# Sample page gathers of the latent attention: the wait on the scores moved from the sixth key chunk to the ninth

## The chip, the cores and the metric

One core of one Trainium2 chip runs the whole kernel. The metric is device time in microseconds (us) of one launch; three runs of the kernel before gave 2556.86, 2560.39 and 2561.03 us, median 2560.39 us. TensorE's granted clock is 0.998 of its full 2.4 GHz over the profiled execution.

## The reference, cut to what matters

One inference step of a two-layer decoder: a prompt group of 256 tokens and a sample group of 8 sequences with 8 new tokens each. Every layer has two feed-forward blocks around a token mixer with three branches: a delta-rule recurrence, a dilated window attention, and a multi-head latent attention. The change touches the third branch, for the samples. Each sample has 2048 past tokens, kept as 16 pages of 128 rows in a pool; a row is 256 latent numbers and 32 rotated key numbers, and a page table says which pages a sample owns.

```python
ckv = cache_mla_ckv[l][page_table].reshape(db, past_len, KV_LORA)       # gathered latents
krope = cache_mla_krope[l][page_table].reshape(db, past_len, DROPE)     # gathered rotary keys
s = (einsum('bqhc,blc->bhql', ql, ckv_all) + einsum('bqhr,blr->bhql', qr, krope_all)) * scale
p = softmax(where(key_rows <= rows, s, -inf))
o_lat = einsum('bhql,blc->bqhc', p, ckv_all)
```

Everything is float32. The latents serve twice: transposed as keys of the scores, and as they stand as values.

## The kernel before, in words

Each engine has a program of its own, written out by hand; they meet only in semaphores. `S["ml_mm"]`, `S["ml_pv"]` and the like are counters, `then_inc` adds to one when an instruction is done, and `wait_ge` holds an engine until a counter has reached a value. No planner reorders anything.

The stage of the samples' latent attention (`ml_sample` in the programs of TensorE, ScalarE and VectorE) loops over the 8 samples, here called sample 0 to 7. For sample b TensorE does in order:

- `ml_scores(b)`, the scores of 64 queries against 2048 keys, in nine chunks `d` of the contracted width: 0 to 3 use the low half of the latents (`KTl`), 4 to 7 the high half (`KTh`), 8 the rotary keys (`KRT`). A chunk is eight calls on 32-row by 64-column tiles, which the trace shows as 16 instructions. All of them accumulate in four PSUM banks. `ml_mm` is raised twice for each sample, after chunk 5 and after chunk 8.
- `by_channel(b-2)`, `ml_own_tokens(b+1)` (the scores against the sample's own new tokens, which raises `ml_s`), `values(b-1)` (32 matmuls of the shares of the last sample with its gathered latents; raises `ml_pv`), and `shares(b, ...)`, which transposes the exponentials of sample b.

VectorE does for sample b: `maximum(b)`, whose large reduction of the scores (L2771) waits for `ml_mm` to be 2(b+1), so for chunk 8, and is followed by four small steps (L2772 to L2775); `own_scores(b+1)` (L2764, waits for `ml_s`); `keys(b+1, 0)`, two transposes (L2716) of the next sample's low latents, which wait until that sample's pages have landed; `result(b-2)`; `own_share(b)` (L2783); `keys(b+1, 1)`, three more transposes; and `divisor(b)`. ScalarE takes the exponentials of sample b when `maximum(b)` is done.

The pages of a sample come by three indirect transfers of GpSimd (POOL): two for the latents (`latents_gathered`, L699, 1 MB each by its tile of 128 x 2048 numbers) and one for the rotary keys (`krope_gathered`, L695, a tile of 128 x 512 numbers). There are four places for pages (`KRc[b % 4]`), so sample b's transfers overwrite sample b-4's pages, which `values(b-4)` read last. GpSimd's loop takes the samples in order. For samples 4 to 7 it waits for `ml_pv` to be b-3, which says that this place is free, and for `ml_mm` to be 2(b-2)+1, chunk 5 of the scores of sample b-2. For samples 2 and 3 it waits for the prompt's outputs and for `ml_mm` to be b: chunk 8 of sample 0 for sample 2, chunk 5 of sample 1 for sample 3. The rotary keys of sample 3 are fetched early, with sample 1. After sample 7 this queue has nothing until the next feed-forward block. SyncE's queue, meanwhile, loads the branch's weights (`br`, `c`) when `ml_pv` is 5, and the first half of the output weights when `ml_mm` is 16.

Of the kernel before, what the change touches and what calls it, by code (L numbers as in the profile page):

```python
# [282 lines left out]
def build(nc, io):  # L283
    SCB, SCC = DH ** -0.5, (DNOPE + DROPE) ** -0.5
    with ExitStack() as ctx:
# [3 lines left out]
        def sem(name):  # L289
            return ctx.enter_context(nc.semaphore(name))  # L290
# [33 lines left out]
        def cut(buf, at, a, b, rows=P):  # L324
# [85 lines left out]
        kr_at = [(big, 3072, big, 5120, big, 7168), (reg, 10720, reg, 12768, reg, 14816), (ring, 9088, h_flat, 0, ring, 11136),  # L410
                 (ring, 0, ring, 2048, ring, 4096)]
        KRc = [[cut(b0, at0, 8, KV_LORA), cut(b1, at1, 8, KV_LORA)] for b0, at0, b1, at1, _, _ in kr_at]
        KRr = [buf[:, at:at + 512] for _, _, _, _, buf, at in kr_at]
        QL = reg[:, 2016:15328].rearrange("p (c n) -> p c n", c=2)
        KTl = [cut(ring, 4608 + 2048 * i, 4, 512) for i in range(2)]
# [20 lines left out]
        S = {n: sem(n) for n in STEPS}  # L436
# [5 lines left out]
        units = weight_units(io)  # L442
        slot_of, before = weight_slots(units)
        uidx = {name: i for i, (name, _) in enumerate(units)}

        heads = [("f1", "gu", u) for u in range(HEAD)]
# [39 lines left out]
        def layer_begun(eng, l):  # L486
            eng.sem_inc(s_arrive, 1)
            eng.wait_ge(s_go, l + 1)
            eng.sem_inc(s_pad, 1)

        def lay(ap, l):
            return ap[bass.ds(l, 1)]
# [167 lines left out]
        @block.gpsimd  # L660
        def _(pool):
            for i in range(8):
                pool.dma_start(ptab[N_PAGES * i:N_PAGES * i + N_PAGES, :], io["page_table"].rearrange("b n -> n b"), allow_slow_non_contiguous=True).then_inc(s_copy, 16)
            pool.wait_ge(s_copy, TABLE)
            for l in range(DEPTH):
                layer_begun(pool, l)

                def copied(first, last):
                    for i in range(first, last):
                        if i:  # L670

                            pool.wait_ge(s_copy, l * (16 * 2 * NB) + TABLE + 16 * i)
                            pool.sem_inc(s_pad, 1)
                        b, n = i // 2, "kv"[i % 2]
                        src = lay(io["cache_swa_" + n], l)[:, b, TS:PAST].rearrange("a r n -> (a r n)")
                        dst = lay(io[f"o_swa_{n}_s"], l)[:, b, 0:PAST - TS].rearrange("a r n -> (a r n)")
                        pool.dma_start(dst.rearrange("(q n) -> q n", q=240),
                                       src.rearrange("(q n) -> q n", q=240)).then_inc(s_copy, 16)

                def copied_in_ffn(f, first):  # L680
                    for i, n in enumerate([u - 1 for u in COPY_GU] + [10 + p for p in COPY_DOWN]):
                        pool.wait_ge(S["gu_prod"], 7 * (SUMS0[f] + n) + P5_)
                        copied(first + i, first + i + 1)

                copied_in_ffn("f1", 0)
                pool.wait_ge(S["pam"], 1)
                copied(COPY_AT[0], COPY_AT[1])
                pool.wait_ge(S["pages_ready"], 1)

                def rows_of(b, i):  # L690
                    return bass.IndirectOffsetOnAxis(ap=pidx[:, i * NB + b:i * NB + b + 1], axis=0)

                def krope_gathered(b):
                    src = io["cache_mla_krope"].rearrange("l n (s r) c -> (l n s) (r c)", s=8)
                    pool.indirect_dma_start(out=KRr[b % 4], out_offset=None, in_=src, in_offset=rows_of(b, 0)).then_inc(s_kr[b % 4], 16)  # L695

                def latents_gathered(b, half):
                    src = io["cache_mla_ckv"].rearrange("l n (s r) c -> (l n s) (r c)", s=16)
                    pool.indirect_dma_start(out=KRc[b % 4][half].rearrange("p n c -> p (n c)"), out_offset=None, in_=src, in_offset=rows_of(b, 1 + half)).then_inc(s_kr[b % 4], 16)  # L699

                for b in range(NB):
                    if b == 0:
                        pool.wait_ge(S["sws_done"], NB)
                    elif b == 1:
                        copied(COPY_AT[1], COPY_AT[2])
                        pool.wait_ge(S["prompt_mm"], 2 * H + 16)
                        pool.wait_ge(S["ml_prep"], 1)
                    elif b in (2, 3):

                        pool.wait_ge(S["prompt_y"], 2 * H)  # L710
                        pool.wait_ge(S["ml_prep"], 1)
                        pool.wait_ge(S["ml_mm"], b)
                    else:

                        pool.wait_ge(S["ml_pv"], b - 3)
                        pool.wait_ge(S["ml_mm"], 2 * (b - 2) + 1)
                    if b < 3:
                        krope_gathered(b)
                    for half in range(2):
                        if (b, half) == (2, 1):  # L720
                            pool.wait_ge(S["pgm"], 24)
                        latents_gathered(b, half)
                    if b == 1:
                        pool.wait_ge(S["pgm"], 20)
                        krope_gathered(3)
                    if b >= 4:
                        krope_gathered(b)
                copied_in_ffn("f2", COPY_AT[2])
                pool.wait_ge(s_copy, l * (16 * 2 * NB) + TABLE + 16 * 2 * NB)
# [2170 lines left out]
```

## Time and profile before

| What | Value |
|---|---|
| Median of three runs | 2560.39 us |
| Profiled execution, its own time | 2568.66 us |
| Its span | 2566.9 us |
| TensorE busy | 2511.7 us (98%) |
| VectorE busy | 1313.2 us (51%) |
| ScalarE busy | 562.6 us (22%) |
| GpSimd busy | 67.7 us (3%) |
| DMA, mean | 197 GB/s |

The span runs from the first to the last instruction; the execution's own time is 1.8 us longer. A matmul's end is modelled, so a busy TensorE may hide short holes. The stage of the samples' latent attention lies near 878 to 970 us for layer 0 and 2148 to 2240 us for layer 1.

### The profile page before, as it was taken

Reading aid. Unit: us, or ns where it says so; the run is one execution under the profiler, and the core shown is the slowest. Engines: PE = TensorE matmul, PEld = TensorE weight load, DVE = VectorE, ACT = ScalarE, POOL = GpSimd, SP = SyncE. Lnnn points to the kernel's source line nnn. Section 1 sums busy time; section 2 is a strip of 40 time slices with the busy share of each in tenths; the row PEclk is TensorE's granted clock in tenths of the full one; section 3 lists DMA queues with packets and bytes.
Section 4 is the critical chain, followed back from the end, with each engine's and each line's share of the span. In section 5 each row is a group of like instructions: output and inputs, shape, how many; then the busy total and the mean of one; then the engine's idle time right before and its main releaser. Section 6 shows DMA issues by size and latency. Waiting matters only on the chain.

```text
span 2566.9 us, 52968 instructions
## 1 busy us (share of the span) xinstructions
PE 2511.7 (98%) x23108; PEld 2047.8 (80%) x23108; DVE 1313.2 (51%) x2839; ACT 562.6 (22%) x1257; POOL 67.7 (3%) x92
## 2 busy tenths in 40 slices
PE   7999999999999999999999999999999999999998
PEld 6999966656666768999999998566666666689998
DVE  5664553435542472765376535533455335637654
ACT  2110231123422222211021102311344222221111
POOL 0000000000000110000000000000000001100000
PEclk9999999999999999999999999999999999999999
DMA  7767661142986553566856686411439764446675
GB/s 251 249 194 246 234 198 67 35 152 109 387 323 231 160 191 131 182 213 212 260 186 217 205 265 240 133 67 68 171 131 390 293 222 163 183 131 197 212 222 160
DMA packets 260709, 505.66 MB, mean 197 GB/s; under 512 B 9792, under 2 KB 198720, under 8 KB 245376
## 3 DMA queue, kind: packets, MB, share of 16 engines
q1 hardware_dynamic: 251776, 330.83, 38.8%
q0 software_dynamic: 8704, 171.45, 18.5%
q8 instruction: 183, 3.00, 0.5%
q14 instruction: 46, 0.38, 0.0%
HBM read 491.95 MB, written 140.85 MB: 247 GB/s over the span
## 4 chain that ended last, share of the span: by engine, by line
PE 89%; DVE 5%; ACT 2%; DMA 1%; another core or an unknown queue 1%; issue 1%; PEld 1%; SPq 0%; DVEq 0%; ACTq 0%
PE ps L742 84%; PE ps L745 5%; DVE big L2716 1%; DMA big<-in_cache_swa_k_dram 1%; DVE ring L2716 1%; ACT big L1890 1%; PEld ps L742 1%; ACT reg L1890 0%; DVE sml L2771 0%; DVE reg L2058 0%; DMA parn<-in_params_dram 0%; DVE reg L2132 0%; DVE x L2050 0%; DVE reg L2650 0%
## 5 line engine op out<-in xcount | busy, mean ns | idle before, releaser
L742 PE MATMUL ps<-reg 128*128 128x160 f32 (+12 forms) x4584 | 513.4, 292 | 1.6 <-DVE reg L2137 1.6
L742 PEld LDWEIGHTS ps<-reg 128*128 128x128 f32 (+5 forms) x4584 | 454.3, 163 | 32.8 <-issue 22.5
L742 PE MATMUL ps<-h,ring 128*128 128x320 f32 (+2 forms) x1984 | 450.0, 378 | 14.7 <-ACT h L1626 13.7
L742 PE MATMUL ps<-reg,ring 128*128 128x160 f32 (+1 forms) x3040 | 458.9, 306 | 0.0
L742 PEld LDWEIGHTS ps<-reg,ring 128*128 128x128 f32 x3040 | 426.1, 189 | 16.4 <-issue 6.2
L742 PEld LDWEIGHTS ps<-h,ring 128*128 128x128 f32 (+1 forms) x1984 | 323.7, 190 | 105.7 <-issue 27.6
L742 PE MATMUL ps<-ring,h 128*128 128x512 f32 (+3 forms) x896 | 247.9, 468 | 0.0
L742 PEld LDWEIGHTS ps<-big,ring 128*128 128x128 f32 (+2 forms) x2016 | 197.3, 168 | 24.8 <-issue 20.5
L742 PE MATMUL ps<-big,ring 128*128 128x160 f32 (+2 forms) x2016 | 214.4, 279 | 0.5
L742 PEld LDWEIGHTS ps<-ring,h 128*128 128x128 f32 (+1 forms) x896 | 101.6, 163 | 76.4 <-issue 61.0
L742 PE MATMUL ps<-big,reg 32*64 32x256 f32 (+8 forms) x2144 | 132.8, 347 | 2.3 <-DVE big L2716 2.3
L742 PEld LDWEIGHTS ps<-big,reg 32*64 32x64 f32 (+4 forms) x2144 | 100.9, 133 | 28.9 <-issue 14.8
L745 PE MATMUL ps<-cst,big 128*128 128x128 f32 (+1 forms) x672 | 98.3, 283 | 16.9 <-ACT big L1890 7.3
L745 PEld LDWEIGHTS ps<-cst,big 128*128 128x128 f32 (+1 forms) x672 | 72.1, 140 | 37.4 <-ACT big L1890 12.4
L1736 ACT ACTIVATE reg<-ps 128x320 f32<-128x320 f32 x40 | 17.5, 437 | 316.3 <-PE ps L742 316.3
L742 PE MATMUL ps<-ring 128*16 128x128 f32 (+3 forms) x1888 | 86.0, 261 | 0.0
L742 PEld LDWEIGHTS ps<-ring 128*16 128x16 f32 (+3 forms) x1888 | 69.7, 111 | 13.9 <-issue 12.8
L745 PE MATMUL ps<-cst,reg 128*128 128x128 f32 (+3 forms) x436 | 71.7, 282 | 5.7 <-DVE sml L2650 2.5
L742 PE MATMUL ps<-ys,ring 128*128 128x320 f32 x256 | 75.4, 440 | 0.2
L2282 DVE TENSOR_TENSOR ys<-ys,ps 128x320 f32<-128x320 f32 x40 | 19.5, 487 | 108.1 <-PE ps L742 108.0
L745 PEld LDWEIGHTS ps<-cst,reg 128*128 128x128 f32 (+3 forms) x436 | 48.9, 140 | 28.1 <-issue 11.8
L742 PE MATMUL ps<-ring,reg 32*64 32x256 f32 (+2 forms) x1312 | 70.0, 374 | 0.0
(322 smaller groups left out, 2658.0 us busy)
## 6 DMA issues: line engine op xcount, KB each, us to landing
out_o_swa_k_s_dram<-in_cache_swa_k_dram POOLq DMA_DIRECT2D x16, 4080.0 KB, 15.5
out_o_swa_v_s_dram<-in_cache_swa_v_dram POOLq DMA_DIRECT2D x16, 4080.0 KB, 14.8
ring<-in_w_in_dram SPq DMA_DIRECT2D x30, 2048.0 KB, 8.6
ring<-in_f_wd_dram SPq DMA_DIRECT2D x32, 1408.0 KB, 7.1
ring<-in_f_wg_dram SPq DMA_DIRECT2D x42, 1024.0 KB, 5.9
ring<-in_f_wu_dram SPq DMA_DIRECT2D x42, 1024.0 KB, 8.9
big<-in_cache_swa_k_dram SPq DMA_DIRECT2D x32, 1024.0 KB, 8.4
ring<-in_cache_swa_v_dram SPq DMA_DIRECT2D x32, 1024.0 KB, 7.3
```

The lines of the kernel that those rows point to most:

```text
L742: return pe.matmul(out, lhsT, rhs, start=first, stop=last, skip_group_check=True)
L745: return pe.transpose(out, in_, ident[0:rows, 0:rows])
L1736: act.activation(GU[u % 2][:, :, 0, 0:HT], summed(X), ACT.Copy).then_inc(S["gu_act"], 1)
L1890: act.activation(KTw[n % 2][:, c, 0:w], ps[:, 4 + c % 2, 0:w], ACT.Copy).then_inc(S["kt_act"], 1)
L2282: dve.tensor_tensor(Vs, Xc, Y, ALU.add).then_inc(S["gu_sum"], 1)
L2716: dve.transpose(out, pages).then_inc(S["ml_keys"], 1)
```

## The change

Two waits of GpSimd's loop get other values; no instruction is added or taken away.

```diff
                     elif b in (2, 3):
 
                         pool.wait_ge(S["prompt_y"], 2 * H)
                         pool.wait_ge(S["ml_prep"], 1)
-                        pool.wait_ge(S["ml_mm"], b)
+                        pool.wait_ge(S["ml_mm"], 2 * (b - 1))
                     else:
 
                         pool.wait_ge(S["ml_pv"], b - 3)
-                        pool.wait_ge(S["ml_mm"], 2 * (b - 2) + 1)
+                        pool.wait_ge(S["ml_mm"], 2 * (b - 1))
```

For sample 2 the value stays 2. For sample 3 it goes from 3 to 4, and for samples 4 to 7 from 2b-3 to 2b-2: the transfers of sample b are released by chunk 8 of the scores of sample b-2, and not by chunk 5 (the sixth of the nine). That is the counter and the value for which VectorE's large reduction of sample b-2 waits.

## Rows read from the trace of the kernel before

**Rows 1.** The page: the span, and the chain that ended last by engine.

```profile
span 2566.9 us, 52968 instructions
...
PE 89%; DVE 5%; ACT 2%; DMA 1%; another core or an unknown queue 1%; issue 1%; PEld 1%; SPq 0%; DVEq 0%; ACTq 0%
```

**Rows 2.** VectorE's waits with no known releaser: us in total, times, longest.

```profile
DVE sml L2771 <- remote: 22.9, 9, 3.2
...
DVE ring L2764 <- remote: 2.5, 7, 0.4
```

**Rows 3.** Order of time, scores' last chunk: start, us, instruction, [idle before].

```profile
892.01 0.64 PE L742 MATMUL ps<-big 32*64 32x256 f32 x16
...
915.73 0.64 PE L742 MATMUL ps<-big 32*64 32x256 f32 x16
...
939.31 0.64 PE L742 MATMUL ps<-big 32*64 32x256 f32 x16
...
949.88 0.64 PE L742 MATMUL ps<-big 32*64 32x256 f32 x16
...
2162.32 0.64 PE L742 MATMUL ps<-big 32*64 32x256 f32 x16
...
2221.38 0.64 PE L742 MATMUL ps<-big 32*64 32x256 f32 x16
...
2232.00 0.69 PE L742 MATMUL ps<-big 32*64 32x256 f32 x16
```

**Rows 4.** Order of time, VectorE's large reduction of samples 1, 3, 5, 6.

```profile
895.08 1.23 DVE L2771 TENSOR_REDUCE sml<-ps 128x1 f32<-128x1024 f32 x1 [3.22 <-remote]
...
918.06 1.23 DVE L2771 TENSOR_REDUCE sml<-ps 128x1 f32<-128x1024 f32 x1 [2.36 <-remote]
...
940.47 1.23 DVE L2771 TENSOR_REDUCE sml<-ps 128x1 f32<-128x1024 f32 x1 [1.18 <-PE ps L742]
...
950.63 1.23 DVE L2771 TENSOR_REDUCE sml<-ps 128x1 f32<-128x1024 f32 x1 [1.05 <-PE ps L742]
```

**Rows 5.** Order of time, GpSimd's gathers beside the scores of samples 1, 3, 5.

```profile
892.22 0.94 POOL L699 DMA_INDIRECT ring<-in_cache_mla_ckv_dram,pidx  x1 [4.16 <-PE ps L742]
893.46 0.94 POOL L699 DMA_INDIRECT ring<-in_cache_mla_ckv_dram,pidx  x1 [0.30 <-issue]
...
915.91 0.94 POOL L699 DMA_INDIRECT reg<-in_cache_mla_ckv_dram,pidx  x1 [8.35 <-PE ps L742]
917.16 0.93 POOL L699 DMA_INDIRECT reg<-in_cache_mla_ckv_dram,pidx  x1 [0.30 <-issue]
918.39 0.95 POOL L695 DMA_INDIRECT reg<-in_cache_mla_krope_dram,pidx  x1 [0.30 <-issue]
...
939.87 0.94 POOL L699 DMA_INDIRECT ring<-in_cache_mla_ckv_dram,pidx  x1 [8.73 <-issue]
```

**Rows 6.** Order of time, TensorE: chunks 4 to 7 and own-token scores, sample 3.

```profile
913.95 1.99 PE L742 MATMUL ps<-big,reg 32*64 32x256 f32 x64 [0.25 <-DVE big L2716]
...
917.22 0.28 PE L742 MATMUL ps<-reg,big 32*64 32x8 f32 x2
```

**Rows 7.** Order of time: own scores beside sample 5, low transposes beside sample 6.

```profile
942.43 0.16 DVE L2764 TENSOR_TENSOR ring<-ps,cst 64x8 f32<-64x8 f32 x1
...
952.78 2.37 DVE L2716 STREAM_TRANSPOSE ring<-ring 128x1024 f32<-128x1024 f32 x2
```

**Rows 8.** Chain of waits, sample 3: start us, us, what.

```profile
920.35 0.17 DVE ring L2764
```

**Rows 9.** The values' matmuls of sample 0 and of sample 1, order of time.

```profile
893.11 4.07 PE L742 MATMUL ps<-big,reg 128*64 128x256 f32 x32
...
905.78 3.67 PE L742 MATMUL ps<-reg 128*64 128x256 f32 x32
```

**Rows 10.** By tensor, issue to landing: the rotary keys, then the latents.

```profile
DMA to landing us min/median/max: 6.5/6.8/7.9
...
DMA to landing us min/median/max: 5.5/7.1/9.1
```

## The prediction

> **What bounds the kernel now.** Read first is the page [rows 1]: TensorE carries 89% of the chain that ended last, VectorE 5%, and "another core or an unknown queue" 1%, which is odd for a kernel on one core. The waits of VectorE say where that is [rows 2]: nine times its large reduction of the scores (L2771) waited for something the profile does not know, 22.9 us in all, and seven times its own-token step (L2764), 2.5 us. Both belong to the stage that the change touches, so the rest is read there, in order of time.
>
> The stage repeats once for each sample; the period is the distance between two last chunks of the scores [rows 3]. In layer 0 it is 10.57 us from sample 5 to 6, but (939.31 - 892.01)/4 = 11.8 us on the four periods before; between samples 3 and 5 it is exactly (939.31 - 915.73)/2 = 11.79 us. In layer 1 the five periods from sample 1 to 6 take 59.06 us, and the next one 10.62 us. So nine periods are about 1.2 us longer than they need to be, and the short ones give TensorE's own pace.
>
> What makes them longer stands in [rows 4]. For sample 6 the reduction begins 0.11 us after the last chunk's end (949.88 + 0.64 = 950.52, then 950.63). For sample 3 the end is 916.37 us and the reduction begins at 918.06, 1.69 us late; for sample 1 it is 895.08 against 892.65, 2.43 us late. The counter for which it waits was raised by then. In exactly these periods GpSimd has just begun its gathers [rows 5]: at 915.91 us, 0.46 us before the last chunk's end, and at 892.22, 0.43 before. For sample 6 there is no gather left. The one mixed case is the best evidence: for sample 5 in layer 0 the gather began late by itself, at 939.87, 0.08 us before the chunk's end (939.95), and the reduction began at 940.47, only 0.52 us late, and the following period was a short one. In layer 1 the gather of the same sample fell as usual, and the period was long. I read this as: a gather that begins on GpSimd while VectorE sits in this wait lengthens the wait. The traces show the coincidence, not the mechanism.
>
> The own-token step is late too: for sample 3 it begins at 920.35 [rows 8], 2.29 us after the reduction began, and for sample 5 only 1.96 after [rows 4, 7]. Its counter was raised at 917.22 + 0.28 = 917.50 [rows 6]. VectorE therefore loses 1.59 us at the reduction (918.06 against 916.37 + 0.10) and 0.33 us behind it, 1.92 us in a period. Without them its loop would take 11.79 - 1.92 = 9.87 us, 0.70 us less than TensorE's 10.57 us: the stage would be bound by TensorE.
>
> **The change, part by part.** *When the gathers start.* Chunks 4 to 7 are the row at 913.95 and chunk 8 that at 915.73 [rows 6, 3], so a chunk takes 1.78/4 = 0.445 us. Chunk 5 ends 3 x 0.445 = 1.34 us before chunk 8, at 915.04, and GpSimd began 0.87 us later [rows 5]. With the new value it begins 0.87 us after chunk 8: at 917.24 in sample 3's terms, with the other two at 918.49 and 919.72 (the spacing of [rows 5]). The reduction begins at 916.47, before any of them.
>
> *What is taken away.* The nine long periods go down to TensorE's pace: 47.30 - 4 x 10.57 = 5.02 us in layer 0 and 59.06 - 5 x 10.62 = 5.96 us in layer 1. Against this I leave 0.4 us in each layer, because the values' matmuls of sample 0 took 4.07 us and those of sample 1 3.67 us [rows 9], and this is TensorE's own time, beside pages that still land. Sum: 10.98 - 0.80 = 10.2 us.
>
> *What is late next on VectorE.* The own-token step would be ready at 916.47 + 1.96 = 918.43, and its counter is raised at 917.50, now 0.26 us into the first gather: the place in which the reduction's counter stood before (0.46 us in). No row shows this wait with a gather started as here, so it is bounded. Lower end: no delay, 0 us, as for sample 5 in layer 0, whose counter also came while gathers ran. Middle: it is held as the reduction was, until 918.06 - 915.91 = 2.15 us after the first gather's start, so until 919.39, 0.96 us late; 0.70 of it is covered by VectorE's slack, 0.26 x 9 = 2.3 us are lost. Upper end: until 920.35 - 918.39 = 1.96 us after the third gather's start, as this very step was held before, worked out below as a rival. I take the lower end, which is nearest to the only row where gathers start this late. A hold further on, at the copy of the own share (L2783), would find the same cover of 0.70 us.
>
> *What the later start costs the transfers.* Nothing is issued twice and no queue gets longer: GpSimd has nothing behind sample 7's gathers until the next feed-forward block, and behind each gather only the next sample's, a period away. The branch's and the output weights on SyncE wait for TensorE's counters and move with it. The data of sample b are wanted by the low transposes during sample b-1; for sample 6 these begin at 952.78, 2.26 us after the last chunk [rows 7, 3], so the deadline is 10.57 + 2.26 = 12.8 us after chunk 8 of sample b-2. The third transfer starts 0.87 + 2.48 us after that chunk and lands at most 7.9 us later, at 11.3 us; the second starts at 2.12 and lands at most 9.1 us later, at 11.2 [rows 10]. Cover 1.6 us (0.6 us if landing were counted from the end of the 0.95 us issue), and then VectorE's 0.70 us. The cost is put at 0. Sample 7's pages share the DMA engines with the branch's weights, as before, so its cover is the thinnest; if it is gone, a microsecond or so is lost in each layer. The wait for `ml_pv` and the overwriting of pages need nothing new, since chunk 8 is later than chunk 5.
>
> **The sum.** The profiled execution took 2568.66 us (span 2566.9, 1.8 around it). Less 10.2 that is 2558.5 us. The median of the three runs is 8.3 us below the profiled execution; the stage is bound by engines and not by what differs there, so the same 10.2 us are taken from 2560.39: 2550.2 us.
>
> **The rivals.**
>
> *The held wait moves on and grows (slower).* Mechanism: what is held is any counter from TensorE to VectorE raised during the gathers, and a counter raised in the first gather is let through 1.96 us after the third's start. Place: L2764. In sample 3's terms it would begin at 919.72 + 1.96 = 921.68, 1.33 us later than now. Seven periods of 11.79 us grow by this, 9.3 us; layer 0's free period from 5 to 6 becomes 13.1, 2.6 us; the two periods after sample 1, whose set has two gathers (release 895.08 - 893.46 = 1.62 us after the last), gain 0.66 each. Sum +10.5 us: 2570.9 us. For it: L2764 was held seven times [rows 2], in the row shown to that distance. Against it: in layer 0 sample 5 it was not, with all three gathers around it. It decides once the hold of this step is longer than 1.92 us, the time that the change gives VectorE back.
>
> *Nothing changes.* The late start is not the gathers' doing, or it comes back in full at another wait of the loop. Time 2560.4 us. For it: no row names the releaser, and the reduction of sample 5 ran beside a gather without being slower (1.23 us [rows 4]). The Trainium skill, "SBUF — State Buffer", section "Who interferes with whom", says that a `tensor_reduce` on VectorE never contends with GpSimd for their shared port pair on this chip, and that an instruction with at most one SBUF input outside the two-port modes doesn't either. By that rule the lateness would not be a lock that the gathers hold, and a later gather would give nothing back: 2560.4 us. The trace agrees on the duration and leaves the late start unexplained. Against this rival stand nine late starts with early gathers [rows 2], an on-time one where no gather is left, and the half-late one in between.
>
> *Held in part.* The middle bound: 10.2 - 2.3 = 7.9 us saved, 2552.5 us.
>
> **How the numbers follow.** The forecast of 2550.2 has a chance of 0.48, the partial hold 0.15, no change 0.19, the slower case 0.18. 0.2% of the time, 5.1 us, is what a measurement of this kernel can tell from no change. Both first cases lie beyond it: faster 0.63, same 0.19, slower 0.18. The forecast's own ends are 2547 us (the 0.4 us for the values go too, and the runs spread by 3 us below their median) and 2553. To hold eight in ten the range takes in the partial hold and no change with its spread, 2547 to 2563 us, and leaves out the slower case.
>
> **What would show it.** Right: the first gather of each sample from 3 on begins about 0.9 us after the last chunk; the reduction begins about 0.1 us after it for all samples, and its waits without a releaser are gone; the periods are near 10.6 us from sample 2 on, 0 to 0.8 us more between 1 and 2; the low transposes wait for no transfer. Wrong: L2764, or L2783, with idle time before it and no releaser, and periods of 11.8 us or more (a hold that moved); low transposes that begin with a DMA as releaser (late pages); the reduction still 1.7 us late with a gather behind it (the gathers were never the cause).

## The result: slower by 0.23%, and the profile after

The changed kernel takes 2566.49 us (median of 13 runs, 2562.59 to 2569.60) beside 2560.71 us before (13 runs, 2556.86 to 2563.57): a ratio of 1.0023, interval 1.0016 to 1.0030. I had forecast 2550.2 us; the range ended at 2563.

The profiled execution of the changed kernel has the span of the one before it, 2566.9 us, and looks, at first, as foretold. First its page, the chain that ended last by engine; the unknown releaser of [rows 1] is gone.

```profile
span 2566.9 us, 52968 instructions
...
PE 94%; ACT 2%; DVE 2%; DMA 1%; issue 1%; PEld 1%; SPq 0%; DVEq 0%; ACTq 0%
```

Then VectorE and GpSimd in order of time beside samples 1 and 3, the answer to [rows 4, 5].

```profile
892.42 1.22 DVE L2771 TENSOR_REDUCE sml<-ps 128x1 f32<-128x1024 f32 x1 [0.90 <-PE ps L742]
...
917.04 1.23 DVE L2771 TENSOR_REDUCE sml<-ps 128x1 f32<-128x1024 f32 x1 [2.01 <-PE ps L742]
...
917.77 0.94 POOL L699 DMA_INDIRECT reg<-in_cache_mla_ckv_dram,pidx  x1 [7.68 <-PE ps L742]
```

Sample 3's last chunk ends at 916.29 + 0.64 = 916.93; the reduction begins 0.11 us later and the gather 0.84 us later. All the late starts of [rows 2] are gone. But TensorE in order of time, the answer to [rows 3], has something that was nowhere before, idle time with no releaser ("issue"):

```profile
891.68 0.64 PE L742 MATMUL ps<-big 32*64 32x256 f32 x16
...
903.23 1.35 PE L742 MATMUL ps<-big,reg 32*64 32x256 f32 x24 [2.06 <-issue]
...
916.29 0.64 PE L742 MATMUL ps<-big 32*64 32x256 f32 x16
926.86 0.64 PE L742 MATMUL ps<-big 32*64 32x256 f32 x16
...
939.14 0.66 PE L742 MATMUL ps<-big 32*64 32x256 f32 x8 [1.10 <-issue]
...
951.42 0.64 PE L742 MATMUL ps<-big 32*64 32x256 f32 x16
...
2177.60 0.87 PE L742 MATMUL ps<-big,reg 32*64 32x256 f32 x19 [1.83 <-issue]
...
2211.53 0.55 PE L742 MATMUL ps<-ring 128*128 128x64 f32 x4 [0.70 <-issue]
```

Undisturbed samples now take 10.57 us (916.29 to 926.86), as forecast. Around these four stops they don't: sample 2's chunk 8 comes 12.6 us after sample 1's. And the clock fell behind two of them; the third number from the right of the next rows, ahead of the DMA share and GB/s, is the granted clock of a stretch (1.00 is 2.4 GHz, 0.50 is 1.2 GHz):

```profile
903.00:907.00 4.00, 3.77 (x53) 2.52 (x54) 1.09 (x1) 0.00 (x0) 0.35 (x1) 0.57 0.01 4
941.00:945.00 4.00, 4.00 (x24) 2.33 (x24) 3.73 (x12) 1.49 (x4) 2.81 (x3) 0.57 0.55 168
```

So in these two profiles the gain on VectorE is nearly used up by the loss on TensorE (samples 1 to 7 of both layers take 136.3 us after and 138.1 before), and the spans are equal. What they don't say is why the timed runs of before have a median 8 us below its profiled execution, while the changed kernel's lies only 2 us below its own (2568.68 us). That was the first thing to find out.

### The profile page after: what moved, and what is told of

Same layout as the page of the kernel before. It is cut to its first block, busy times and chain, and to the rows that moved or that the text cites. A ratio compares the mean times of both kernels' runs of the same rounds, so it can differ in the third digit from the quotient of the medians.

```text
span 2566.9 us, 52968 instructions
## 1 busy us (share of the span) xinstructions
PE 2513.3 (98%) x23108; PEld 2050.3 (80%) x23108; DVE 1312.8 (51%) x2839; ACT 563.1 (22%) x1257; POOL 67.9 (3%) x92
## 4 chain that ended last, share of the span: by engine, by line
PE 94%; ACT 2%; DVE 2%; DMA 1%; issue 1%; PEld 1%; SPq 0%; DVEq 0%; ACTq 0%
PE ps L742 88%; PE ps L745 6%; DMA big<-in_cache_swa_k_dram 1%; PEld ps L742 1%; ACT big L1890 1%; ACT reg L1890 0%; DMA ring<-in_f_wu_dram 0%; DVE reg L2058 0%; DVE reg L2132 0%; DVE x L2050 0%; DVE reg L2650 0%; DVE ring L2571 0%; DVE reg L2621 0%; ACT big L1640 0%; ACT L1849 0%
```

## The experiments

They were run in four sets, each on one chip together with the kernel before. The kernel before took 2571.49 us (median) in the first, 2559.96 in the second, 2560.55 in the third and 2570.55 in the fourth: it has two levels, and a set lies on one of them. The profile of before that the prediction reads (2568.66 us) lies outside the 13 timed runs, and near the upper level.

**1. The kernel before, again (set one).**

> The kernel before, unchanged, once more. Theory A (the profiled execution of before was not a typical one): its profile took 2568.7 us where its other runs took 2557 to 2564; if the nine late starts of the large reduction (22.9 us of waits with no known releaser) are what made it long, a second profile near 2560 us shows few or none of them, and sample periods of 10.6 us. Rival B (the late starts belong to the kernel): the second profile shows about nine of them again, and the difference of 8 us lies elsewhere. Time: ratio 1.000 within 0.1% in both.

Measured: 2571.40 us, ratio 0.9999 (0.9990 to 1.0007). Its profile has the late starts:

```profile
DVE sml L2771 <- remote: 24.4, 9, 4.6
DVE ring L2764 <- remote: 2.1, 6, 0.4
```

For this level rival B holds: they are the kernel's.

**2 and 3. Only sample 3 moved; only samples 4 to 7 moved (set one).** Each is one of the two lines of the change.

```diff
-                        pool.wait_ge(S["ml_mm"], b)
+                        pool.wait_ge(S["ml_mm"], 2 * (b - 1))
```

> Only the wait of sample 3 is changed (ml_mm 4 and not 3); samples 4 to 7 as before. Theory F: in the changed kernel TensorE stood still without a releaser for 2.1 us in layer 0 and 1.8 us in layer 1 just before the last chunk of sample 2, about 10 us after the gathers of sample 3 began 1 us later; if this first move is what does it, this kernel has most of the change's 5.8 us, about +4 us. Rival G: the cost grows with the number of moved gathers, one of five in each layer: +1 us. If the late starts of VectorE are real, the two of sample 1 go, -1.5 us.

```diff
-                        pool.wait_ge(S["ml_mm"], 2 * (b - 2) + 1)
+                        pool.wait_ge(S["ml_mm"], 2 * (b - 1))
```

> Only the waits of samples 4 to 7 are changed; sample 3 as before. Theory F (first move): about +2 us, the rest of the 5.8. Rival G (all moves alike): +4.6 us. Theory A and B: the late starts of the reduction beside samples 2 to 5 are gone from the profile in either case, that beside sample 1 stays if it is real.

Measured: 2570.53 us (0.9995, 0.9987 to 1.0004) and 2564.42 us (0.9972, 0.9963 to 0.9982). Neither theory F nor G foresaw a gain of 7 us, against a before of 2571.49. The profiles explain it: with sample 3 alone moved, six late starts remain of nine and TensorE stops for 1.51 and 1.83 us; with samples 4 to 7 moved only the two late starts beside sample 1 remain, and TensorE stops for 0.83 and 0.97 us.

**4. Gathers as early as their place is free (set one).**

```diff
                         pool.wait_ge(S["ml_pv"], b - 3)
-                        pool.wait_ge(S["ml_mm"], 2 * (b - 2) + 1)
```

> The wait on the scores is taken out for samples 4 to 7: their gathers start as soon as the values' matmuls have freed the place, some 4 us before chunk 5. If what matters is only that gathers run beside chunk 8 and the large reduction (my first theory), the late starts go and this is 5 to 8 us faster than the profiled before would say. If the transfers' lateness is the cost of the change, this is equal to before or faster by 1 to 2 us. If the transfers themselves stop TensorE's instruction supply wherever they lie, it is within 3 us of before, with stops at other places in the profile.

Measured: 2578.03 us (1.0028, 1.0017 to 1.0039), 6.5 us slower. None of the three expectations foresaw that. The late starts beside samples 2 to 5 are gone, but TensorE stops ten times for 8.0 us together. My first theory alone is refuted: where the gathers lie beside the reduction is not all that matters. The ten stops are not of one kind. Two (1.57 and 1.53 us, at sample 2's chunk 8) end 1.3 to 1.4 us after a block of TensorE's instructions has landed, like those explained under runs 5 and 6. The other eight, 4.9 us together, lie at no such place: each ends 1.7 to 1.8 us after the start of a sample's third gather. What they wait for is not shown; it looks as if what made VectorE's starts late here reaches TensorE itself.

**5 and 6. The changed kernel and before once more (set two).**

> The changed kernel once more, beside before. The kernel before had a median of 2560.7 us where the change was measured and of 2571.5 us in the first set of experiments. Theory C (the result hangs on how fast the chip's transfers run against its engines): where before takes about 2571 us, the changed kernel is faster than before by 2 to 5 us, because the kernel that changes samples 4 to 7 alone was 7 us faster there; where before takes about 2561 us it is slower by 6 us as measured. Rival D: the change of sample 3 is the bad part and adds 10 us or more to the part from sample 4 on everywhere; then it is slower than before by 3 to 6 us in both.

> The kernel before, for a trace from the same conditions as the changed kernel beside it. Theory A: if its median is near 2561 us here, its trace shows few late starts of the reduction and sample periods of 10.6 us. Theory B: the late starts are there whatever the median, eight or nine of them.

Measured: 2565.84 us (1.0022, 1.0013 to 1.0032) and 2561.07 us (1.0003, 0.9994 to 1.0012). Theory A holds. C and its rival D both foresaw the changed kernel's time on this level; set four decides between them. The second profile is what the timed runs of before look like on the lower level; TensorE, VectorE and GpSimd beside sample 3, in order of time:

```profile
913.39 0.64 PE L742 MATMUL ps<-big 32*64 32x256 f32 x16
...
914.14 1.23 DVE L2771 TENSOR_REDUCE sml<-ps 128x1 f32<-128x1024 f32 x1 [1.47 <-PE ps L742]
...
913.58 0.93 POOL L699 DMA_INDIRECT reg<-in_cache_mla_ckv_dram,pidx  x1 [7.67 <-PE ps L742]
...
923.96 0.64 PE L742 MATMUL ps<-big 32*64 32x256 f32 x16
```

The gather begins 0.45 us before the last chunk's end (914.03), as in [rows 5], and yet the reduction begins 0.11 us after it. There is no late start, and the period is 10.57 us. On this level the loss that the change was to take away isn't there. The nearness of gather and wait is thus not enough to make the wait late.

The stops have their cause in the same two traces. The trace shows a DMA queue of kind "instruction" (q8) with 183 packets of 16 KB in a run. TensorE has 46,216 matmuls and weight loads and 730 instructions of its sequencer on record, 256.5 for each packet; and counted over these 46,946 records the four stops stand, in both profiles of the changed kernel, at numbers 16578, 17857, 40130 and 41409: 5 x 256 less one apart in each layer, and 92 x 256 apart between the layers. So I take a packet of q8 for a block of 256 instructions of TensorE. Here are the queues of the changed kernel between 895.1 and 901 us, and then between 901 and 902 us (packets, MB, share):

```profile
q0 software_dynamic: 277, 2.07, 96.1%
...
q8 instruction: 1, 0.02, 6.4%
q0 software_dynamic: 11, 0.02, 6.2%
```

The pages (q0) keep the 16 engines busy for 96% of the time until 901, and the block of instructions is moved only as their last packets go, from 901.09 to 902.12 us. TensorE stood still from 901.62 to 903.40, 1.28 us past the block's landing (the other stops of these two profiles end 1.3 to 1.5 us past the landing of a block):

```profile
903.40 0.91 PE L742 MATMUL ps<-big,reg 32*64 32x256 f32 x24 [1.78 <-issue]
```

In before (run 6) the last packet of sample 3's pages ends at 900.22 and not 901.48, and the same block lands at 900.53; no stop is recorded. From 904.24 us on, behind the stop, the clock is at 1.2 GHz for 6.8 us, and the 32 values' matmuls of sample 1 take 5.49 us where they take 3.67 in before; the clock rows have the columns of those above:

```profile
905.00:907.00 2.00, 2.00 (x23) 1.42 (x8) 1.37 (x2) 0.00 (x0) 0.69 (x1) 0.50 0.00 0
907.00:909.00 2.00, 2.00 (x11) 1.30 (x13) 1.86 (x6) 1.46 (x4) 1.39 (x3) 0.50 0.45 82
...
907.34 5.49 PE L742 MATMUL ps<-reg 128*64 128x256 f32 x32
```

**7 and 8. TensorE's blocks shifted (set two).** 128 satisfied waits ahead of everything, in before and in the changed kernel.

```diff
-            pe.wait_ge(s_once, ONCE)
+            for _ in range(1 + 128):
+                pe.wait_ge(s_once, ONCE)
```

> The kernel before with 128 more waits, satisfied at once, in TensorE's program before its first matmul, where it still waits for weights. Theory F (TensorE stops where its next block of instructions, 256 to a packet, has not come because the pages' packets are ahead of it): the stops move by about 128 instructions, those near sample 2's chunks 6 and 7 go, others appear about a third of a sample further, and the time moves by 1 to 5 us either way. Rival: the stops belong to the operands or the semaphores; then they stay at the same matmuls, and the time is that of before within 0.1%.

> The changed kernel with the same 128 waits. Theory F: the stops of 2.1 us (layer 0) and 1.8 us (layer 1) just before sample 2's last chunk are gone from there; the difference to pad128_before is another than that between the two kernels without the waits, by 2 us or more. Rival: the stops stay where they are, and the difference between the two is unchanged.

Measured: 2560.08 us (1.0003, 0.9994 to 1.0012) and 2566.34 us (1.0026, 1.0015 to 1.0038). The instruction count went from 52,968 to 53,032, so only 64 were added. The places moved as theory F says: the stops before sample 2's chunk 8 are gone, and the longest now stand a sample later, here in chunk 7 of sample 3. Counted with the 64 added records, they stand at the same place of a block of 256 as before.

```profile
915.01 0.44 PE L743 MATMUL ps<-big,reg 32*64 32x256 f32 x4 [1.42 <-issue]
```

The rival (stops bound to operands or semaphores) is out. But the difference of the two kernels stayed, 6.3 us, as the rival had said, and the shift alone changed the time of before by 0.1 us, not by 1 to 5. That part of both expectations was wrong. My reading, not tested further, is that whichever matmul a block begins with, one of the bursts meets it.

**9 and 10. The first raise of the counter after chunk 6, after chunk 7 (set three).** All five moved sets start 0.45 and 0.89 us later than before; the change is 1.34.

```diff
-                    if d in (5, 8):
+                    if d in (6, 8):
```

(and `(7, 8)` for the other)

> The kernel before with the first raise of ml_mm after chunk 6 and not after chunk 5, so all five moved gather sets start 0.45 us later than before and 0.9 us earlier than in the changed kernel. Theory F (the pages' packets keep TensorE's next block of instructions back, and it stops once the block comes later than it is wanted): the delay of 0.45 us uses up part of the lead; before has no stop, the changed kernel stops of 1.8, 1.0, 1.6 and 1.0 us, so here 0.9 us less of each: 0.9, 0.1, 0.7 and 0.1 us, and with little or no low clock behind them the time is 1 to 3 us above before where before takes 2560 us. Rival (an on-off effect of sharing one counter value with VectorE): time of before within 0.1%. Where before takes 2571 us (late starts of the reduction) it is faster by 5 us or more.

> The same with the raise after chunk 7, 0.89 us later than before and 0.45 us earlier than in the changed kernel. Theory F: stops about 0.45 us shorter than in the changed kernel, 1.3, 0.6, 1.1 and 0.5 us; 3 to 5 us above before where before takes 2560 us. Rival (shared counter value): time of before.

Measured: 2561.39 us (1.0002, 0.9993 to 1.0011) and 2562.82 us (1.0006, 0.9997 to 1.0015). With chunk 5 at 1.0000 and chunk 8 at 1.0022 to 1.0023 (from other sets) this is a curve that bends upward: the first 0.45 us of lateness cost 0.8 us of time or nothing, the last 0.45 us about 3.5 us. Theory F had the direction, but too much time: 1 to 3 us and 3 to 5 us, against 0.8 and 2.3 measured. The stops in the stage grow with the lateness:

| First raise after | stops in the stage, us (times) | sample 1 to 7, layers 0 + 1, us |
|---|---|---|
| chunk 5 (run 6) | none | 64.1 + 63.9 |
| chunk 6 | 1.7 (3) | 65.2 + 63.9 |
| chunk 7 | 4.0 (4) | 66.0 + 65.7 |
| chunk 8 (run 5) | 5.3 (4) | 70.0 + 65.9 |

(The last column is the distance between the rows of chunk 8 of samples 1 and 7. Each row is one profile, and that of chunk 7 is the slowest of its kernel's 11 runs, 2567.78 us beside a median of 2562.82, so its last column is above the typical one.) The rival, a switch that depends on sharing one counter value with VectorE, foresaw the time of before for both; the stops of the table speak against it, the two times alone don't reach beyond their intervals.

**11 and 12. Few pages (set three).** For samples 4 to 7 the latents' gathers bring one page each and not eight; the other latents of these samples are stale.

```diff
                 def latents_gathered(b, half):
+                    if b >= 4:
+                        few = lay(io["cache_mla_ckv"], l)[:, 8 * b + half].rearrange("a s c -> (a s) c")
+                        pool.dma_start(KRc[b % 4][half][:, 0, :], few).then_inc(s_kr[b % 4], 16)
+                        return
```

> The kernel before, but for samples 4 to 7 each of the two latent transfers brings one page, 0.125 MB, by a plain transfer from the same queue and not 1 MB by a gather; the rest of the latents is left as it stands. Waits, matmuls and the order are those of before. Theory F: TensorE is at its own pace already (10.57 us a sample) where before takes 2560 us, so this is within 1 us of before, apart from HBM time given back elsewhere.

> The changed kernel with the same small transfers for samples 4 to 7; sample 3 is gathered whole. Theory F: without the long bursts of packets TensorE's blocks come in time; its stops beside sample 5 (layer 0) and sample 5 or 6 (layer 1) are gone, those before sample 2's last chunk stay, as sample 3's pages are whole. Of the 5.9 us between the two kernels the part behind sample 3 goes, some 2 to 3 us, and 2 to 4 us stay. Rival (the wait itself or the later start of GpSimd costs the time): the difference to few_pages_before stays at 5.9 us.

Measured: 2559.75 us (0.9993, 0.9984 to 1.0002) and 2561.24 us (1.0000, 0.9991 to 1.0009). The waits are those of the two kernels, and the difference has shrunk from about 6 us (in the other sets; the changed kernel was not timed in this one) to 1.5 us. Beside samples 5 and 6 no stop is left; the two before sample 2's chunk 8, with sample 3 gathered whole, stay at 1.5 and 1.6 us. More of the cost went than I had said (2 to 3 us): here the clock kept 2.4 GHz through both stages, and the few-pages version of before has stops of 1.0 and 0.5 us at these places. So it is not the wait itself that cost the time but the transfers that it releases: above all their bytes, though the edit also puts plain transfers in the place of indirect ones, and the pair doesn't tell the two apart.

**13 to 16. The upper level again (set four).** The changed kernel, its two parts, and the raise after chunk 6.

> The changed kernel again. If before takes about 2571 us in this set: theory C (the change takes the late starts away and puts TensorE's stops in their place) gives a time 2 to 5 us below before, as the kernel that moves samples 4 to 7 alone was 7 us below. If before takes about 2560 us: 5 to 6 us above it, as in the two sets before.

> Only samples 4 to 7 moved. At a before of 2571 us: 7 us below it again. At 2560 us theory F gives the stops beside sample 5 in each layer, 1.0 us each, and perhaps one stretch at low clock behind them, 1.7 us: 2 to 4 us above before. Rival: none of the cost is here, time of before.

> Only sample 3 moved. At 2571 us: 1 us below before again. At 2560 us theory F gives the stops before sample 2's last chunk, about 1.5 us in each layer, of which 0 to 0.3 us was there before, and low clock behind the first: 2 to 4 us above before; with the other part the two make up the 5.8 us.

> The first raise of ml_mm after chunk 6, all five sets moved by 0.45 us. At 2560 us: within 0.1% of before, as in the last set. At 2571 us: if late starts need a gather that begins 0.4 to 0.5 us before chunk 8's end, here it begins at that end; then they are gone, and without TensorE's long stops this is the fastest of all, 8 to 11 us below before.

| Kernel | time, us | ratio to before (2570.55 us) |
|---|---|---|
| changed | 2566.10 | 0.9978 (0.9968 to 0.9987) |
| samples 4 to 7 moved | 2564.84 | 0.9972 (0.9960 to 0.9983) |
| sample 3 moved | 2571.33 | 1.0002 (0.9993 to 1.0011) |
| raise after chunk 6 | 2561.49 | 0.9965 (0.9952 to 0.9979) |

Theory C holds and D is out: the changed kernel is 4.5 us below before here. Samples 4 to 7 alone give 5.7 us (7 foreseen), sample 3 alone nothing that can be measured (1 foreseen), the raise after chunk 6 9.1 (8 to 11 foreseen). The changed kernel takes 2566 us on both levels, and the raise after chunk 6 takes 2561.4 and 2561.5 us: the two levels are a matter of the kernel before, and of its late starts. The profile of the raise after chunk 6 on this level has no wait with an unknown releaser (beside sample 1 the reduction still begins 0.6 us after the last chunk's end, in both layers), and its longest stop in the stage is 0.96 us. It is the best version: no difference from before is measured on the lower level, and it is 9 us faster on the upper, by five runs.

## Why the prediction was wrong

**The late starts.** They were there, and were taken for something that every run has. They belong to the profile's level, not to that of the timed runs. The step that failed is in the sum: "The median of the three runs is 8.3 us below the profiled execution; the stage is bound by engines and not by what differs there, so the same 10.2 us are taken from 2560.39." What differed was this stage. On the lower level it takes 128.1 us in both layers together (table), on the trace I read it took 138.1 (68.45 + 69.68, samples 1 to 7). The 8.3 us between profile and median were most of the forecast gain, already missing. The clue was in the numbers: a profiled execution 7.6 us above the highest of the three runs shown.

One reading of the late starts was wrong as well: "The counter for which it waits was raised by then." The trace keeps the time of every raise, though the views show only the releaser. For sample 3 the last chunk's matmuls end at 916.37 by their modelled end, `ml_mm` is raised at 918.04, and the reduction begins 0.02 us later; TensorE's next two raises come 1.83 and 2.76 us after their matmuls. There are 25 such late raises in the stage, as in run 1, and none in run 6, where `ml_mm` is raised 0.08 us after the end. So VectorE starts as soon as it may: what is late are TensorE's raises, while its matmuls are recorded at their usual pace.

**When the gathers start, and what that takes away.** Right: 0.84 us after chunk 8 against 0.87, the reduction 0.11 us after it, undisturbed periods of 10.57 us, no hold moved on to L2764 or L2783. The slower rival that I priced (2570.9 us) didn't happen, and the slower result has another cause. On the upper level the sign of the forecast holds: 4.5 us less, where I had 10.2. TensorE's stops in the stage, 5.7 us in the profile of run 13, can account for the rest.

**"What the later start costs the transfers".** I put 0 there, and this is the second step that failed. The landing of the pages was right; no transpose waited for them. I asked who waits for the pages, and not who waits behind them. TensorE's next block of instructions does, and it had no room. Counted from the row of sample 1's chunk 8, TensorE came to the end of its block after 9.61 us (901.62 - 892.01, where it stopped), and it goes on 1.28 us after the next one lands. In before that landed after 8.70 us (900.53 - 891.83), so could be used after about 10.0: the period there is already 10.78 us and not 10.57. With the change it landed after 10.11 us, 1.41 later, and all of that is seen in the stop: the block could be used 11.39 us after the row, 1.78 after it was wanted.

**The sum on the lower level,** from the profiles of runs 5 and 6. The stage grew from 128.1 to 135.9 us, by 7.9. Of this 5.3 us are the four stops, 1.78 + 1.03 in layer 0 and 1.56 + 0.96 in layer 1; the other 2.5 us are left for the matmuls at 1.2 GHz, of which the values' matmuls of sample 1 alone are 5.49 - 3.67 = 1.8. The two spans (2566.5 and 2560.5 us) differ by 6.0, so outside the stage the changed run was 1.9 us shorter. Such stretches of low clock come and go between runs there too (run 6 has one more of 3.4 us, at 1992.8 us), and I take this for their scatter, not for an effect. The medians of the 13 runs each in the section on the result differ by 5.8 us.

**Left open.** What makes TensorE's raises late, and why a set has them or not. A gather that begins 0.4 to 0.5 us before the last chunk's end goes with them on the upper level (none of an unknown releaser with the raise after chunk 6 or 8), and does nothing on the lower. The four sets ran on four different chips, two on each level, so the level may belong to the chip; no chip was measured twice, so no run shows it. Which of the two parts of the change costs how much on the lower level was not timed either; the few-pages pair only leaves about 1.5 of 6 us to sample 3.

## What to carry to other kernels

A profile is one execution: where its time lies outside the timed runs, first ask which of its stalls the timed runs can't have, and take only the rest as the gain. A "remote" releaser on a kernel of one core is a question to the trace: was the waiting engine late, or the raise? When a burst of transfers is moved, look at everything that shares the DMA engines with it, the engines' own instruction packets first, and not only at who needs the data. A release point that can be put at several places is worth a sweep: here one step of 0.45 us gained 9 us on the upper level and cost nothing measurable on the lower, and three steps gained 4.5 and cost 6.

## What the runs showed of the hardware

A 16 KB packet of TensorE's instructions took 0.9 to 1.4 us, but where it met 2 MB of gathered pages it went through with the last of them (901.09 us, in a burst that ended at 901.48), and TensorE went on 1.3 us after its landing. Behind some stops the granted clock fell to 1.2 GHz for 3.4 to 6.8 us: those of 2.06, 1.78 and 1.10 us in layer 0 of the two changed runs above. Behind others it didn't: 1.83 and 1.56 us in layer 1 of the same runs, and 1.51 us in layer 0 with the raise after chunk 7. So the length of the stop alone doesn't decide it. In the two profiles of the kernel before on the upper level, 25 counter raises of TensorE came 1.5 to 3.5 us after the modelled end of the matmuls that make them, while matmuls went on being recorded. The Trainium skill, "SBUF — State Buffer", section "Who interferes with whom", has it that DMA never contends with a compute engine; no run here contradicts it for operands, but through the instruction packets a gather did stop TensorE. And the same binary had two levels 0.4% apart, at a granted clock of 0.996 to 0.999 on both.
